# Attention tile 1 of the second head group: values as weights, four heads a visit, result turned

## What is computed

```python
p = masked_softmax(q @ k.T * scale + bias, mask)   # per head and branch
o_b = g_cmp * (p_cmp @ v_cmp) + g_sel * (p_sel @ v_sel) + g_win * (p_win @ v_win)
mix = concat([rms_norm(o_a, grp_norm_mla), rms_norm(o_b, grp_norm_nsa)])
x = x + mix @ w_o
x = x + square(relu(rms_norm(x, ln2_g) @ w_up)) @ w_down
```

## Time and profile before

| | |
|---|---|
| time, median of 3 runs (us) | 645.41 (645.12 to 646.32) |
| span of the profiled execution (us) | 643.3 |
| TensorE products busy | 632.1 us, 98% |
| DVE busy | 497.3 us, 77% |
| ACT busy | 399.1 us, 62% |
| units of the second group, about | 172 to 308 us |
| `sel` and `win` of tile 1: value products | 253 to 285 us |
| MLP | 316 us to the end |

### The profile page before, as it was taken

One profiled execution on the slowest core, in us unless ns is written; L12 is line 12 of the kernel. 1 busy time (PEld: TensorE's weight loads), 2 busy tenths in 40 slices (PEclk: granted clock), 3 DMA queues, 4 the chain that ended last, 5 costly groups with the idle time before them and its releaser, 6 DMA issues.

```text
span 643.3 us, 11728 instructions
## 1 busy us (share of the span) xinstructions
PE 632.1 (98%) x4153; PEld 560.3 (87%) x4153; DVE 497.3 (77%) x913; ACT 399.1 (62%) x791; POOL 171.9 (27%) x236
## 2 busy tenths in 40 slices
PE   7999999999999999999999999999999999999998
PEld 4999788887789888887999999999998788888886
DVE  6665766589887878897885787777768999897676
ACT  6864675567897647657447666756647555664561
POOL 5656656434412202212110011110111221222200
DMA  9871729998988955995372687788877899999984
GB/s 337 311 268 71 261 72 356 290 292 207 263 255 274 343 178 173 286 288 106 67 198 99 170 230 213 195 230 196 214 179 168 201 245 224 225 239 269 261 258 150
DMA packets 34507, 142.50 MB, mean 222 GB/s; under 512 B 5159, under 2 KB 5543, under 8 KB 33488
## 3 DMA queue, kind: packets, MB, share of 16 engines
q1 hardware_dynamic: 22688, 83.72, 37.4%
q0 software_dynamic: 10208, 34.88, 29.8%
q10 hardware_dynamic: 1552, 23.14, 9.6%
HBM read 139.57 MB, written 65.06 MB: 318 GB/s over the span
## 4 chain that ended last, share of the span: by engine, by line
PE 91%; DVE 4%; ACT 2%; issue 1%; DMA 1%; SPq 0%; ACTq 0%; DVEq 0%
PE bank L2108 15%; PE bank L2109 15%; PE bank L2110 15%; PE bank L2502 7%; PE bank L2504 7%; PE bank L2503 7%; PE bank L2128 7%; PE bank L2337 3%; PE bank L2280 2%; PE bank L2319 2%; PE bank L2434 2%; PE bank L2433 2%; PE bank L2432 2%; PE bank L2291 1%; PE bank L2292 1%
## 5 line engine op out<-in xcount | busy, mean ns | idle before, releaser
L868 POOL DMA_DIRECT2D down_sums<-w_down x64 | 50.0, 781 | 235.0 <-PE bank L2504 143.0
L1393 DVE TENSOR_TENSOR w_lo<-raw,w_hi 128x1024 fp32r<-128x1024 f32 (+3 forms) x70 | 80.9, 1169 | 26.5 <-ACT w_hi L965 26.1
L2108 PE MATMUL bank<-w_hi,act_hi 128*128 128x512 f32 (+3 forms) x224 | 89.2, 398 | 3.2 <-DVE w_lo L1393 3.0
L965 ACT ACTIVATE w_hi<-raw 128x1024 fp32r<-128x1024 f32 (+3 forms) x70 | 68.1, 991 | 34.1 <-DMA raw<-w_pairs 27.3
L2109 PE MATMUL bank<-w_lo,act_hi 128*128 128x512 f32 (+3 forms) x224 | 79.7, 356 | 0.0
L2110 PE MATMUL bank<-w_hi,act_lo 128*128 128x512 f32 (+3 forms) x224 | 79.7, 356 | 0.0
L1119 ACT ACTIVATE p_buf<-s_buf,stats 128x128 f32<-128x128 f32 (+3 forms) x96 | 53.8, 561 | 32.4 <-PE bank L2128 17.3
L1354 ACT ACTIVATE w_hi<-raw 128x1024 fp32r<-128x1024 f32 x31 | 32.8, 1058 | 35.7 <-DMA raw<-down_sums 18.1
L2108 PE MATMUL bank<-w_hi,s_all 128*128 128x512 f32 x140 | 54.6, 390 | 0.0
L2109 PE MATMUL bank<-w_lo,s_all 128*128 128x512 f32 x140 | 54.5, 389 | 0.0
L2110 PE MATMUL bank<-w_hi,s_all 128*128 128x512 f32 x140 | 54.5, 389 | 0.0
(11 more groups left out here) (317 smaller groups left out, 1833.6 us busy)
## 6 DMA issues: line engine op xcount, KB each, us to landing
down_sums<-w_down ACTq DMA_DIRECT2D x32, 512.0 KB, 6.3
down_sums<-w_down POOLq DMA_DIRECT2D x64, 256.0 KB, 5.9
raw<-down_sums SPq DMA_DIRECT2D x32, 512.0 KB, 5.3
up_sums<-w_pairs POOLq DMA_DIRECT2D x28, 512.0 KB, 9.8
raw<-up_sums SPq DMA_DIRECT2D x28, 512.0 KB, 4.8
raw<-weights SPq DMA_DIRECT2D x26, 512.0 KB, 5.7
up_sums<-w_pairs SPq DMA_DIRECT2D x16, 512.0 KB, 6.6
raw<-w_down SPq DMA_DIRECT2D x16, 512.0 KB, 5.3
```

What stands on the lines that cost most here:

```text
L868: pool.dma_start(sums_dram[k, rows_], a["w_down"][SUMS[m][1], step, rows_], accum_op=ALU.add, max_dma_last_dim=4096).then_inc(*sum_added[k ...
L965: ins = act.activation(hi[:, 0:width], raw[:, n % RAW, 0:width], ACT.Copy)
L1393: ins = dve.tensor_tensor(lo[:, 0:width], raw[:, n % RAW, 0:width], hi[:, 0:width].bitcast(F32), ALU.subtract)
L2108: pe.matmul(dst, a_h, w_h, start=start, stop=False, skip_group_check=onto)
```

## The change

Tile 1 of `sel` and `win` of the second group takes the paired form: the order of its heads goes by pairs (0, 4, 1, 5, ...), `paired` holds for it, and with that follow the visits of four heads at steps 40, 45, 49 and 54, the copy to `o_t` at steps 46 and 55, the four transposes at steps 47 and 56, and `out_row` at steps 48 and 57 (before: 46 and 55). Tile 1 of the first group stays as it was. What builds on it moves by one step: square sum, turn and split of tile 1's mix, its two output projections (u 64, 65, 69, 70), the scaled rows of tile 3's second norm (DVE at 55 and 56), their turn (58), their copies (59, 61), and turn and copies of tile 2's (66; 67, 68). DVE waits for the last value product of `win` tile 1 before it writes the rows of tile 3's norm, since the eight places of the probabilities reach into them.

```diff
-                    ("sel", 1, range(4)), ("cmp", 2, [0]), ("sel", 1, range(4, HEADS)),
-                    ("win", 1, range(4)), ("cmp", 1, [0]), ("win", 1, range(4, HEADS)),
+                    ("sel", 1, PAIRED[:4]), ("cmp", 2, [0]), ("sel", 1, PAIRED[4:]),
+                    ("win", 1, PAIRED[:4]), ("cmp", 1, [0]), ("win", 1, PAIRED[4:]),
...
-WO_UNITS = [21, 22, 24, 25, 26, 27, 28, 30, 31, 32, 33, 34, 35, 37, 38, 39, 43, 44, 46, 47, 51, 52, 55, 56, 63, 64, 68, 69]
+WO_UNITS = [21, 22, 24, 25, 26, 27, 28, 30, 31, 32, 33, 34, 35, 37, 38, 39, 43, 44, 46, 47, 51, 52, 55, 56, 64, 65, 69, 70]
...
-LN2_AT = {3: (50, 54, 57), 2: (59, 62, 65)}
-KEEP_AT = {3: (58, 60), 2: (66, 67)}
+LN2_AT = {3: (50, 55, 58), 2: (59, 62, 66)}
+KEEP_AT = {3: (59, 61), 2: (67, 68)}
...
 def paired(m):
 
-    return OUTS[m][0] != "cmp" and OUTS[m][1] >= 2
+    return OUTS[m][0] != "cmp" and OUTS[m][1] >= (2 if OUTS[m][0] == "mla" else 1)
...
 MIX_SQUARE, MIX_TURN, MIX_HI, MIX_LO = ({N_MLA + 29 + d: 3, N_MLA + 37 + d: 2, N_MLA + e: 1}
-                                        for d, e in ((7, 57), (10, 60), (11, 61), (12, 62)))
+                                        for d, e in ((7, 58), (10, 61), (11, 62), (12, 63)))
...
                     if n - N_MLA == LN2_AT[t][1]:
                         dve.wait_ge(*gain2_in.at())
+                        if t == 3:
+                            dve.wait_ge(*mixed.at(LAST_OF[OUTS.index(("win", 1))]))
                         ln2_rows(t, slice(0, 512))
```

## The result

The changed kernel took 653.17 us (median of 4 executions, 652.34 to 653.9) against 645.41 us. The measured ratio is 1.0107, 95% interval 1.0083 to 1.0132; the two medians alone give 1.0120. By the medians that is 7.8 us slower, where 0.9 us was forecast. The span of the profiled execution was 652.1 us against 643.3 us.

A forecast was written before the change was run, and what follows sets the result against it. TensorE mostly bounds, but ACT's lateness at 289 us counts: square sum 3.1 us back less 1.2 us, up products 0.9 us later, 643.3 + 0.9 = 644.2 us, plus 2.1 gives 646.3 us. Range 643.9 to 647.7 us; no-change bounds 644.1 and 646.7 us.

The forecast's parts named there:

- The chain: Behind step 56's projection, DVE does residual, norm rows, scores and closing, 3.5 us; ACT's square sum begins 1.8 us later.
- the last paragraph of the prediction: Signs expected: DVE idle 1 us or more before step 56's residual, ACT waiting for `o_nsa`, MLP length unchanged within 0.3 us.
- TensorE's lead at step 56: TensorE was to end step 56's projection 1.2 us ahead of before, not 1.6 us.
- the `cmp` work that was to run without waiting: With projections now at steps 64 and 65, TensorE would first do a `cmp` score and value product without waiting.
- the term of the visits: Tile 1's value products on TensorE: 6.6 us removed, four visits at 1.18 us added, 4.7 us.
- The 0.43 us at 264.95 us: TensorE's wait for DVE's copy of u 39's probabilities, 0.43 us, was to go, since visits ask two steps later.
- the bank of u 46: TensorE's `cmp` product at step 50 may wait for its bank, at most some 0.5 us, if DVE is behind.
- "TensorE's work from there to the up products is the same as before": From the mix split on, TensorE's work stays unchanged; up products begin 0.9 us later.
- (a): Rival: TensorE passes its whole saving of 1.2 to 1.6 us on, 643.8 to 644.2 us; chance 0.28.
- (b): Rival: gains and losses cancel, the late square sum costing 1 us less, 645.1 to 645.7 us; chance 0.18.
- (c): Rival: more waits at steps 49 and 50 and ACT copies leave the square sum 3 us late, 647.9 us; chance 0.12.
- the copies on ACT: Two bank copies to `o_t` at steps 46 and 55: nothing taken, at most 0.3 us if step 47 lacks slack.

The follow-up runs named there:

- Experiment 2: Changed kernel, with DVE closing tile 1's window branch at step 56 instead of 57 and doing tile 3's norm rows ahead of the residual: 650.20 us.
- experiment 1: Changed kernel, with the score products of units 58 to 62 done six times over to keep TensorE busy: 652.54 us.
- experiment 3: Kernel before, with only the change's moved lists of due steps; products in the old form, window branch closed at step 55: 649.73 us.
- experiment 5: Kernel before with the moved lists, DVE splitting tile 1's mix ahead of closing tile 0's selected branch at step 63: 647.85 us.
- experiment 7: Changed kernel, with six filler products ahead of step 64's projection and score products of units 59, 60, 61 repeated three, three and four times: 652.73 us.
- experiment 14: Changed kernel, window closing and norm rows ahead of the residual at DVE's step 56, tile 1's mix split first at step 63: 651.04 us.
- experiment 11: Kernel before, with five fills of a free buffer on DVE at the end of its step 57: 648.52 us.
- experiment 12: Kernel before, with five fills of a free buffer on DVE at the end of its step 48: 649.95 us.
- experiment 8: Both branches of tile 1 paired, lists as in the kernel before except tile 3's norm rows, window branch closed at step 56 after the norm rows' turn: 647.11 us.
- experiment 9: Both branches paired with the lists of before, window branch closed at DVE's step 56 and selected branch at 47: 646.23 us.
- experiment 10: Both branches paired, lists of before, closings at DVE's steps 47 and 56, tile 3's norm rows ahead of the window closing: 646.60 us.
- experiment 13: Changed kernel, with DVE splitting tile 1's mix ahead of closing tile 0's selected branch at step 63: 651.22 us.
- experiment 6: Kernel before with the moved lists, plus six filler products of 128 columns ahead of step 64's projection: 649.46 us.

## Why the prediction was wrong

**The direction and the place were right.** The chain was projection, residual, norm rows, scores, closing, ACT's square sum, 3.5 us; it measured 289.22 to 292.70 us, 3.5 us. DVE showed the idle time ahead of the residual (1.86 us), ACT the wait for `o_nsa` (1.48 us), as the last paragraph of the prediction asked for. Experiment 2 shows that it matters: 3.0 us. The size failed: 7.8 us instead of 0.9 us. Four steps of it were wrong: TensorE's lead, the `cmp` work that was to run without waiting, the moved lists, and the clock, for which there was no term.

**TensorE's lead at step 56 was taken as 1.2 us and was -0.3 us.** The projection ended at 289.22 us instead of 288.95 us. First the term of the visits: from the start of a visit to the next instruction it was 1.02 to 1.03 us for three of them and 1.17 us for the one at step 49, with 0.2 us around each, some 5.0 us for four instead of 4.7 us. Two of them on the chain:

```profile
260.07 1.05 PE bank L2339 x16
...
268.61 1.02 PE bank L2339 x16
```

Then the waits. The 0.43 us at 264.95 us that I counted as gone did not go: TensorE waits for DVE's copy of the probabilities in the next turn instead, for the bank that the copy empties (0.52 us at 264.73 us). And the bank of u 46 cost 0.65 us, more than the 0.5 us that the walk had as its most. The lead, 1.1 us at the projection of step 44, was used up by these. The rule of the Trainium skill that I weighed (TensorEngine Tiling (Array Packing), Overview, Theoretical Speedup: up to 2x) is farther from the rows than my own number: four heads took 1.02 us and 0.2 us around them, against 4 x 0.41 us.

**"TensorE does a `cmp` score and a value product first, without waiting" was wrong.** I followed DVE's split of tile 1's mix to step 63 and noted that it is one more split there, but did not ask who waits for it. It is the first projection of tile 1, at step 64, 1.73 us in experiments 1, 2 and 3. Mending it gave 1.9 us in experiment 5. In the changed kernel itself there is no such wait: the low clock brought TensorE there late.

**"TensorE's work from there to the up products is the same as before" left the lists no price of their own.** Moved alone, with every product as before, they cost 4.3 us (experiment 3): the 1.73 us above, waits of 0.71 and 1.18 us for ACT ahead of it, and the low clock behind them.

The 0.9 us of the forecast, the 1.5 us by which the lead was less, and the 1.7 us of this wait are 4.1 us, near the 4.3 us of experiment 7. That sum is made afterwards.

**The clock had no term.** The rows had it at 1.00 throughout, and the prediction took that as given for a kernel that it expected to hold TensorE up. It is an estimated 1 to 3 us of the 7.8 us (experiment 7). It is not what takes the time out of the range: with a full clock the shift is still 4.3 us, which is some 649.7 us, against 646.7 us at the most. Nothing in the trace of before shows its price. The Trainium skill has the mechanism in its page TensorE: Matmul & The Clock Gate (Part 1: The HAM clock gate): the clock follows how busy TensorE has been. The traces agree, since every fall in the units told of here stands behind idle time of TensorE. By it the forecast would have needed a rival at the lower level for some microseconds, and I gave none. The same page of the Trainium skill (Why this matters for your kernels) warns of long idle gaps between matmuls. Here the measurement goes further: in this kernel the fall came behind four short waits, 3.7 us together, and in experiment 14 behind one of 1.14 us.

**The rivals.** (a) and (b) fell with ACT's wait. (c), more waits, was the nearest with 647.9 us. Of what it counts, the wait for the bank of u 46 was there (0.65 us, where it had 0.5 us) and the lead at step 56 was gone; the visit of step 49 was only 0.15 us longer than the others, and no row here tells whether the copies on ACT cost the 0.3 us.

**What stays open**: how the loss divides in the changed kernel is known only to a microsecond or two, since its executions all had the low clock and the fills cost time of their own; and which of the lists' moves makes TensorE's two waits at 293 to 297 us was not tried one by one. Nor is it known why the clock is low in one execution of a program and not in the next.

## What to carry to other kernels

When work is moved to a later step, ask of every piece who waits for it and what its engine will do in the place that it leaves: here DVE idled 1.86 us where the work had been, and then did it on the path. Where a forecast adds idle time on TensorE in the midst of dense work, give the fall of its clock a rival with a price: beside the waits it was next to nothing in experiment 11, 1.4 us in 12 and up to 3 us in the changed kernel. Weigh a form that saves 0.3 to 1 us on one engine against what comes behind it: here its result passes through two more engines and comes a step or two later, and in experiments 8 to 10 the paired form was never better than the plain one.

## What the runs showed of the hardware

- The clock fell behind 3.7 us of waits spread over 7 us, none over 1.2 us (the changed kernel), behind one of 2.4 us and behind one of 2.1 us (experiments 11 and 12), and behind much less: waits of 0.43 and 1.11 us (13), and one of 1.14 us after 5 us in which TensorE was busy throughout (14).
- At its lower level it stayed for 3.4 us (12), 7 us (11) and some 10 us (the changed kernel), though TensorE was busy nearly all the while from the fall on; in 13 it stayed for some 14 us, with TensorE idle for 1.3 us of them.
- The same stretch brought it down in some executions of a program and not in others: 1.000 to 0.989 in seven executions of experiment 6, 4.3 us between them. The kernel before had mean clocks of 0.990 to 0.995 in 7 of 69 executions, the changed kernel 0.989 to 0.992 in all four.
- In six of the profiled executions (experiments 2, 6, 7, 9, 10 and 14) it fell early too: 0.57 from 12 to 16 us (0.79 in 2), and all that follows came some 0.9 us later (0.3 us in 2). The trace of the kernel before does not have it; some of its executions without a trace have the mean clock of 0.997 that goes with it.
- Two heads side by side, in halves of the array, with 128 columns streaming: 16 recorded instructions in 1.02 us, against 4 x 0.41 us for the same products the other way round.
